# One more K pair of every SwiGLU up strip by seven products instead of eight: four pairs, at groups 5, 7, 10 and 12, where there were three

## The reference

```python
def swiglu(x, w_up, w_down):
    g, u = jnp.split(x @ w_up, 2, axis=-1)
    return (jax.nn.silu(g) * u) @ w_down

h = h + 0.5 * rms_norm(swiglu(rms_norm(h, ffn1_pre[l]), ffn1_up[l], ffn1_down[l]), ffn1_post[l])
h = h + rms_norm(mix, mix_post[l])
h = h + 0.5 * rms_norm(swiglu(rms_norm(h, ffn2_pre[l]), ffn2_up[l], ffn2_down[l]), ffn2_post[l])
```

## Time and profile before

| | |
|---|---|
| median of 3 runs | 2365.75 us (2365.57 to 2366.02) |
| the profiled execution | 2365.93 us, span 2364.2 us |
| PE busy | 2349.9 us (99%), 10579 matmuls |
| DVE busy | 1823.2 us (77%) |
| ACT busy | 1265.4 us (54%) |
| POOL busy | 207.0 us (9%) |
| DMA | 481.64 MB, mean 204 GB/s |

### The profile page before, as it was taken

The page is one execution under the profiler, slowest core; times in us unless marked ns, Lnnn a source line. Parts: engine busy times, 40 slices in busy tenths (PEclk is TensorE's granted clock), DMA queues, the critical chain, the costliest instruction groups (busy, mean ns, idle before and its releaser), DMA issues. The chain is left out here.

```text
span 2364.2 us, 34093 instructions
## 1 busy us (share of the span) xinstructions
PE 2349.9 (99%) x10579; PEld 1938.5 (82%) x10579; DVE 1823.2 (77%) x2163; ACT 1265.4 (54%) x1519; POOL 207.0 (9%) x402
## 2 busy tenths in 40 slices
PE   9999999999999999999999999999999999999998
PEld 7888888888888888888888888888888888888887
DVE  5999999978876655656675767665799999997886
ACT  6555555555545554454555544544655555555553
POOL 1212112110000000000000000000021212111000
PEclk9999999999999999999999999999999999999999
DMA  7666676665676565565565566666666666666665
GB/s 236 218 212 206 216 222 215 220 214 192 207 242 210 159 182 172 160 188 158 178 200 192 195 195 203 194 240 198 204 210 225 213 214 207 218 213 214 205 204 196
DMA packets 267183, 481.64 MB, mean 204 GB/s; under 512 B 21217, under 2 KB 54673, under 8 KB 265457
## 3 DMA queue, kind: packets, MB, share of 16 engines
q1 hardware_dynamic: 252752, 453.04, 59.5%
q0 software_dynamic: 14192, 27.73, 3.5%
q10 hardware_dynamic: 176, 0.07, 0.0%
HBM read 462.93 MB, written 6.29 MB: 198 GB/s over the span
## 5 line engine op out<-in xcount | busy, mean ns | idle before, releaser
L1382 ACT ACTIVATE w_hi<-w_raw 128x1024 fp32r<-128x1024 f32 (+1 forms) x848 | 857.4, 1015 | 926.1 <-PE acc L843 627.9
L1778 DVE TENSOR_TENSOR w_lo<-w_raw,w_hi 128x1024 fp32r<-128x1024 f32 (+1 forms) x848 | 984.2, 1164 | 420.0 <-ACT w_hi L1382 415.5
L841 PE MATMUL acc<-w_hi,xT_hi 128*128 128x512 f32 x1376 | 540.9, 393 | 1.2 <-DVE w_lo L1778 1.0
L843 PE MATMUL acc<-w_hi,xT_lo 128*128 128x512 f32 x1376 | 535.9, 389 | 0.0
L842 PE MATMUL acc<-w_lo,xT_hi 128*128 128x512 f32 x1376 | 535.7, 389 | 0.0
L841 PEld LDWEIGHTS acc<-w_hi,xT_hi 128*128 128x128 f32 x1376 | 258.3, 188 | 56.7 <-issue 3.0
L843 PEld LDWEIGHTS acc<-w_hi,xT_lo 128*128 128x128 f32 x1376 | 258.3, 188 | 54.4
L842 PEld LDWEIGHTS acc<-w_lo,xT_hi 128*128 128x128 f32 x1376 | 258.4, 188 | 52.2
L753 POOL DMA_DIRECT2D act_raw<-blocks x352 | 174.9, 497 | 736.3 <-DVE blocks L2114 646.9
L841 PE MATMUL acc<-w_hi,act_hi 128*128 128x512 f32 x560 | 218.2, 390 | 0.1
L842 PE MATMUL acc<-w_lo,act_hi 128*128 128x512 f32 x560 | 217.9, 389 | 0.0
(11 more groups left out here) (321 smaller groups left out, 2866.0 us busy)
## 6 DMA issues: line engine op xcount, KB each, us to landing
w_raw<-in_ffn_up_dram SPq DMA_DIRECT2D x352, 512.0 KB, 4.2
w_raw<-in_ffn_down_dram SPq DMA_DIRECT2D x176, 512.0 KB, 4.2
w_raw<-in_w_gate_dram SPq DMA_DIRECT2D x96, 512.0 KB, 4.4
w_raw<-in_w_in_dram SPq DMA_DIRECT2D x72, 512.0 KB, 3.7
w_raw<-in_w_in_dram SPq DMA_DIRECT2D x128, 256.0 KB, 3.0
w_raw<-in_w_ret_out_dram SPq DMA_DIRECT2D x32, 512.0 KB, 4.1
w_raw<-in_w_out_dram SPq DMA_DIRECT2D x32, 512.0 KB, 4.5
act_raw<-blocks POOLq DMA_DIRECT2D x352, 32.0 KB, 3.8
```

The costliest lines, as they stand in the source:

```text
L841: pe.matmul(pair[m][:, :], xh, wh, start=(first and kk == 0), stop=False)
L843: mm = pe.matmul(pair[m][:, :], xl, wh, start=False, stop=(last and kk == KG - 1))
L1382: act.activation(w_hi[:, s, cols], w_raw[:, s, cols], ACT.Copy).then_inc(w_rounded, 1)
L1778: dve.tensor_tensor(w_lo[:, s, cols], w_raw[:, s, cols], w_hi[:, s, cols].bitcast(f32), ALU.subtract).then_inc(w_split, 1)
```

## The change

`QUADS` gets a fourth pair, so K pairs 4 to 7 go by seven products, the gate groups standing at 5, 7, 10 and 12 of a pass. The plain groups are reordered: gate groups at 0 to 3, up groups at 4, 9, 14 and 15. The first plain up group, which opens the up half's accumulator, now stands ahead of the first pair, and so the wait for that accumulator moved from the first pair to it. The pair at groups 7 and 8 lies in slots 3 and 0, so the helpers that address its blocks wrap around (`quad_block`, `outer_blocks`, `t_row`). The token sums cover eight K tiles instead of six; `s_hi` moves to the place of `h`, which needs a wait in ScalarE for the store of `h` in the second block. The two places of the sums of weights are used in turn (0, 1, 0, 1).

```diff
-QUADS = ((5, 6, 5), (9, 10, 6), (12, 13, 7))
-PLAIN_GATE = ((0, 0), (1, 1), (2, 2), (3, 3), (4, 4))
-PLAIN_UP = ((7, 0), (8, 1), (11, 2), (14, 3), (15, 4))
+QUADS = ((5, 6, 4), (7, 8, 5), (10, 11, 6), (12, 13, 7))
+PLAIN_GATE = ((0, 0), (1, 1), (2, 2), (3, 3))
+PLAIN_UP = ((4, 0), (9, 1), (14, 2), (15, 3))
...
-        s_hi = sb("s_hi", [P, 4, NQUAD, P], f32r, at=s_x + 16 * NQUAD * P)
+        s_hi = sb("s_hi", [P, 4, NQUAD, P], f32r, at=x_at - 4 * MT * D)
...
-        T_SLOT = (1, 0, 1)
+        T_SLOT = (0, 1, 0, 1)
...
+        PARKED = 16 * MT * 2
...
+        def t_row(j, y):
+
+            swapped = QUADS[j][0] % SLOTS == SLOTS - 1 and y < 2
+            return 1 - y if swapped else y
...
-                for b, tiles in ((2, range(0, 2)), (3, range(2, S_TILES))):
+                for b, tiles in ((2, range(0, 4)), (3, range(4, S_TILES))):
...
-                if first:
-                    pe.wait_ge(acc_read[pair_of(sec, 1)], strip_in_pair(sec, i, 1) + 1)
                 pe.wait_ge(w_split, group(sec, i, nu) + 1 + SLOTS)
                 pe.wait_ge(s_split, f + 1)
-                three(upper[0][:, :], *s(3), *w(nu, 1), first, False).then_inc(w_used, 1)
+                three(upper[0][:, :], *s(3), *w(nu, 1), False, False).then_inc(w_used, 1)
...
+                            if k == 0:
+                                pe.wait_ge(acc_read[pair_of(sec, 1)], strip_in_pair(sec, i, 1) + 1)
...
+                        if f == 1:
+                            act.wait_ge(h_parked, PARKED)
...
-            def quad_blocks(j):
-
-                s = QUADS[j][0] % SLOTS
-                return w_raw[:, s:s + 2, :].rearrange("p s (kk n) -> p (s kk) n", kk=KG)
+            def quad_block(j, y):
+
+                s = (QUADS[j][0] + y // KG) % SLOTS
+                return w_raw[:, s, y % KG * STRIP:(y % KG + 1) * STRIP]
+
+            def outer_blocks(j):
+
+                first, last = [KG * ((QUADS[j][0] + y // KG) % SLOTS) + y % KG for y in (0, 3)]
+                lo, hi = min(first, last), max(first, last)
+                return w_raw[:, :, :].rearrange("p s (kk n) -> p (s kk) n", kk=KG)[:, lo:hi + 1:hi - lo, :]
...
-                dve.wait_ge(t_used, quad(f, i, j) + (2 if j == 0 else 1))
+                dve.wait_ge(t_used, quad(f, i, j) + 1)
                 dve.wait_ge(w_landed[ng % SLOTS], group_landed(sec, i, ng))
                 dve.wait_ge(w_landed[nu % SLOTS], group_landed(sec, i, nu))
-                dve.tensor_tensor(t_pair(t_raw, j, 0), b[:, 0::3, :], b[:, 2:3, :].broadcast_to([P, 2, STRIP]),
+                dve.tensor_tensor(t_pair(t_raw, j, 0), outer_blocks(j), b2.broadcast_to([P, 2, STRIP]),
                                   ALU.add).then_inc(t_summed, 1)
```

More of the change, by code:

```diff
@@ L254, in hybrid_trunk @@
         s_lo = sb("s_lo", [P, 4, NQUAD, P], f32r, at=s_x)
-        s_hi = sb("s_hi", [P, 4, NQUAD, P], f32r, at=s_x + 16 * NQUAD * P)
-        assert s_x + 32 * NQUAD * P <= r_end
+        s_hi = sb("s_hi", [P, 4, NQUAD, P], f32r, at=x_at - 4 * MT * D)
+        assert s_x + 16 * NQUAD * P <= r_end
         h_scaled = sb("h_scaled", [P, S_TILES * P], f32, at=r_hi)
@@ L962, in tt @@
                 def tt(y):
-                    return t_hi[:, T_SLOT[j], y, :], t_lo[:, T_SLOT[j], y, :]
+                    return t_hi[:, T_SLOT[j], t_row(j, y), :], t_lo[:, T_SLOT[j], t_row(j, y), :]
                 if first:
@@ L1121, in swiglu @@
                                     mm = three(acc[pair_of(sec, 1)][m][:, :], xT_hi[:, k + kk, rows], xT_lo[:, k + kk, rows],
-                                               w_hi[:, s, cols], w_lo[:, s, cols], m == 1 and k + kk == 0,
+                                               w_hi[:, s, cols], w_lo[:, s, cols], k + kk == 0,
                                                n == 2 * GD - 1 and kk == KG - 1)
@@ L1592, in swiglu @@
                                 if n == 12:
-                                    wait_quad_used(act, f, NST - 1, 1)
+                                    wait_quad_used(act, f, NST - 1, 2)
                                 hidden_hi(f, n - 12)
@@ L1951, in token_sums @@
                 dve.tensor_tensor(s_raw[:, 3, :, :], a12, s_raw[:, 1, :, :], ALU.add).then_inc(s_summed, 1)
-            def quad_blocks(j):
-                s = QUADS[j][0] % SLOTS
-                return w_raw[:, s:s + 2, :].rearrange("p s (kk n) -> p (s kk) n", kk=KG)
+            def quad_block(j, y):
[5 more added lines that the diff above has]
+                return w_raw[:, :, :].rearrange("p s (kk n) -> p (s kk) n", kk=KG)[:, lo:hi + 1:hi - lo, :]
             def sum13(f, i, j):
                 sec, (ng, nu, k) = f"up{f}", QUADS[j]
-                b = quad_blocks(j)
-                dve.wait_ge(t_used, quad(f, i, j) + (2 if j == 0 else 1))
+                b2 = quad_block(j, 2).rearrange("p (a n) -> p a n", a=1)
+                dve.wait_ge(t_used, quad(f, i, j) + 1)
                 dve.wait_ge(w_landed[ng % SLOTS], group_landed(sec, i, ng))
                 dve.wait_ge(w_landed[nu % SLOTS], group_landed(sec, i, nu))
-                dve.tensor_tensor(t_pair(t_raw, j, 0), b[:, 0::3, :], b[:, 2:3, :].broadcast_to([P, 2, STRIP]),
+                dve.tensor_tensor(t_pair(t_raw, j, 0), outer_blocks(j), b2.broadcast_to([P, 2, STRIP]),
                                   ALU.add).then_inc(t_summed, 1)
             def sum24(f, i, j):
-                b = quad_blocks(j)
                 t = t_raw[:, T_SLOT[j], :, :]
                 dve.wait_ge(t_summed, 3 * quad(f, i, j) + 1)
-                dve.tensor_tensor(t[:, 2, :], t[:, 0, :], b[:, 3, :], ALU.add).then_inc(t_summed, 1)
+                dve.tensor_tensor(t[:, 2, :], t[:, t_row(j, 0), :], quad_block(j, 3), ALU.add).then_inc(t_summed, 1)
                 dve.wait_ge(t_summed, 3 * quad(f, i, j) + 2)
-                dve.tensor_tensor(t[:, 3, :], t[:, 2, :], b[:, 1, :], ALU.add).then_inc(t_summed, 1)
+                dve.tensor_tensor(t[:, 3, :], t[:, 2, :], quad_block(j, 1), ALU.add).then_inc(t_summed, 1)
             def down_sum13(f, i, j):
```

## The result

| | before | after |
|---|---|---|
| median | 2365.89 us (2365.57 to 2367.36, 4 runs) | 2413.82 us (2413.40 to 2415.56, 4 runs) |
| the profiled execution | 2365.93 us, span 2364.2 us | 2413.59 us, span 2411.8 us |

The ratio after to before is 1.0203, with a 95% interval of 1.0185 to 1.0220: slower by 2.0%. Forecast were 2416 us. The first line is the page's busy time by engine, which answers to the earlier trace rows.

The account below looks back on a forecast made before the run. PE bound the kernel before; with the change DVE's list no longer fits under PE and a loop sets the pass. 44.8 + 5.5 = 50.3 us on the 2364.2 us span gave 2414.5, forecast as 2416 us, range 2402 to 2430.

Parts of the forecast that it names:

- The matmuls saved: Up passes: the fourth pair puts 21 matmuls in place of 24; PE alone needs 40.80 us, 0.68 us less a pass.
- DVE no longer fits under PE: Up passes: the pair adds 4.21 us to DVE's 38.81, giving 43.02 us against 40.80 us of PE work.
- The walk: Steps from B (PE's first matmul of group 0) to the next B, forecast at B+43.72, 2.24 us later than before.
- the two decisive `t_lo`: Second `t_lo` of the pairs at 5 and 10, starting at B+16.60 and B+30.72; PE waits 0.8 and 1.9 us.
- the loop: Chain from one B to the next: DVE makes `w_lo` of the next group 3 only after PE has used group 15.
- PE idle of 2.9 us a pass: PE waits for `t_lo` in two places, the third sums' product of the pairs at 5 and 10.
- 44.8 us for 20 passes: Up strips: each pass's next B comes 2.24 us later, over 20 passes.
- 5.5 us for the first passes: Each block's first pass: larger token sums delay `w_lo` of group 4, 2.5 us a block; with transposes 5.5 for both.
- PE stays the bound: Rival for the up passes: DVE catches up, the kernel gets faster, 2353 us; 3 in 100.
- the sides cancel: Rival: PE's saving and DVE's extra balance within 0.2%, a pass of just 41.5 us; 1 in 100.
- Loads late: Rival: loads reach the pairs' sums late, 0.5 to 1.45 us a pass, 2426 to 2445 us; 10 in 100.
- The clock: Rival: waits drop PE to 1.2 GHz, up to 11.6 us a pass; beyond the first passes, 2 in 100.

Follow-up runs that it names:

- e5_free: Kernel after, with `w_lo` of groups 4, 5, 9, 10 and 14 subtracting only 32 of 1024 columns in every pass; 2356.46 us, ratio 0.9956.
- b2_dup4: Kernel before, with four more 128x1024 DVE subtractions in each pass of `up0`, results unread; 2391.87 us against 2367.17 us of before on that chip.
- e2_outside: Kernel after, with `w_lo` of group 15 cut to 32 of 1024 columns, behind the second `t_lo` of the pair at 10; 2413.95 us.
- e8_short: Kernel after, with `w_lo` of the next pass's group 2 cut to 32 of 1024 columns; 2414.05 us, ratio 1.0204.
- e3_inside: Kernel after, with `w_lo` of group 9 cut to 32 of 1024 columns, between the second `t_lo` of the pairs at 5 and 10; 2397.05 us.
- e1_order: Kernel after, with the second `t_lo` of the pairs at 5 and 10 moved ahead of the next pair's sums on DVE; 2424.09 us, ratio 1.0244.
- e9_swap5: Kernel after, with only the second `t_lo` of the pair at 5 moved ahead of the next pair's sums; 2433.56 us, ratio 1.0289.
- e7_both: e1_order with, besides, `w_lo` of the next pass's group 2 cut to 32 columns as in e8_short; 2416.20 us, ratio 1.0214.
- b1_dup2: Kernel before, with two more 128x1024 DVE subtractions in each pass of `up0`, results unread; 2370.08 us against 2367.17 us of before on that chip.
- e4_pool3: e1_order with `sum24` of the pairs at 7, 10 and 12 done by GpSimd instead of DVE; 2520.24 us, ratio 1.0655.
- e6_first: Kernel after, with ACT making `s_hi` one turn later, behind `w_hi` of the next pass's group 3, in each first strip; 2411.80 us.

## Why the prediction was right

- **The matmuls saved, 0.68 us a pass.** Count and size held: 10523 matmuls, and 40.80 us for a pass in e5_free, as forecast.
- **DVE no longer fits under PE.** Held: the pass of 43.63 us less DVE's two waits of 0.30 is 43.03 us; 43.02 was forecast (the window shows 42.72 busy, since it leaves out the short gaps). That a load of this size is enough for the loss, without a fourth pair, is shown by b2_dup4; that the pair costs nothing else is shown by e5_free. The steps of 1.14, 1.33 and 0.60 us were right, and the strided sum costs no more than a plain one: 212.78 to 213.92 for `sum13` of the pair at 10, 204.04 to 205.18 for that of the pair at 7, whose blocks lie in slots 3 and 0; the 0.3 us that the forecast allowed for the stride came from no row. (N+151)/0.96, which it takes from the Trainium skill's page "VectorE: DVE Perf Modes", section "The TRN2 errata", gives nanoseconds and not cycles: 1224 ns for 1024 columns, and the rows have 1.22 us.
- **The walk.** Forecast were B+16.60 and B+30.72 for the two decisive `t_lo`, and B+43.72 for the next B. Measured: B+16.58, B+30.66, B+43.63. That these places bound the pass and not merely lie on the way is shown by e2_outside, e8_short (outside: nothing) and e3_inside (inside: nearly all of it). What the prediction did not say is how near the next bound was. It named DVE's sum only as the lower end of the range; e1_order and e9_swap5 show that with the loads and `t_hi` that a late DVE gets late it lies at 43.4 to 43.9, beside the loop. In the kernel after the two already touch: in some passes of `up1` DVE does not wait at 3' at all (1866.13 and 1909.70). Relieving the loop alone, by the order, buys nothing; e3_inside took work out of both.
- **PE idle of 2.9 us a pass.** The places were right, the way of counting was not. The brackets give 0.70 + 1.52 = 2.2 us. The other 0.6 are the modelled length of the matmul ahead of each wait (0.39 for a step of 0.23) and the slow first one behind it (0.34 to the next start): 2 x (0.16 + 0.11) = 0.54.
- **44.8 us for 20 passes.** It was 42.6: ten of 43.65 - 41.48 = 2.17 us and ten of 43.57 - 41.48 = 2.09. A pass was sized 0.07 to 0.15 us too long, 0.06 of it in DVE's steps up to the pair at 10.
- **5.5 us for the first passes.** The parts in the first strip stood where forecast, as its rows of ACT and DVE show, which answer to the earlier trace rows:

```profile
57.76 1.92 ACT L1580 ACTIVATE s_hi<-s_raw 128x2048 fp32r<-128x2048 f32 x1 [1.71 <-DVE s_raw L1960]
...
60.66 1.23 DVE L1787 TENSOR_TENSOR w_lo<-w_raw,w_hi 128x1024 fp32r<-128x1024 f32 x1 [1.79 <-ACT w_hi L1389]
61.80 2.28 DVE L2150 TENSOR_TENSOR s_lo<-s_raw,s_hi 128x2048 fp32r<-128x2048 f32 x1
...
66.67 1.18 DVE L1787 TENSOR_TENSOR w_lo<-w_raw,w_hi 128x1024 fp32r<-128x1024 f32 x1
```

  `s_hi` was forecast at 57.7, `w_lo` of 4 near 66.8. By the shifts above, the first passes cost 24.4 - 21.7 = 2.7 us in `up0` (2.75 forecast) and 23.3 - 20.9 = 2.4 us in `up1`, 5.1 together. The transposes were priced too high: ACT's `w_hi` behind them, released by PE, starts 0.08 us later (54.99 against 54.91), where 0.27 was forecast.
- **Together.** 42.6 + 5.1 = 47.7 us, where the span grew by 47.6 and 50.3 was forecast. Both terms were a little too large, so the hit is not one error making up for another.
- **The rivals.** *PE stays the bound* and *the sides cancel* did not come. *Loads late*: none in the loop of the kernel after; the thin margin was enough, and a little delay of the list eats it up (e1_order, e7_both, e9_swap5). *The clock*: the forecast priced it as 51 matmuls behind each fall; it is about eight. It fell in one place of the strips of after, in the first pass of `up1` behind the longest wait (granted clock 0.50 from 1753 to 1755 us):

```profile
1751.93 0.50 PE L939 MATMUL bank<-t_hi,s_hi 128*128 128x512 f32 x1 [3.08 <-DVE t_lo L2174]
1752.27 0.44 PE L940 MATMUL bank<-t_lo,s_hi 128*128 128x512 f32 x1
1752.51 0.63 PE L941 MATMUL bank<-t_hi,s_lo 128*128 128x512 f32 x1
1752.93 0.63 PE L939 MATMUL acc<-t_hi,xT_hi 128*128 128x512 f32 x1
...
1766.01 0.50 PE L939 MATMUL bank<-t_hi,s_hi 128*128 128x512 f32 x1
```

  Eight steps of 0.43 us are 1.6 us more, and yet they cost this kernel nothing. The last row is the pair at 10's third sums' product in the same pass, which elsewhere waits 1.5 us; here PE comes to it later and there is no bracket (this is the wait that is missing to 40). A fall behind the wait at the pair at 5 is paid out of the wait at the pair at 10. In e9_swap5 the falls came behind the last wait of a pass, and counted in full. The first pass of `up0` has a wait as long (3.06 us, at 77.98) with no fall behind it.
- **Left open.** Why e7_both gave back 0.4 us a pass and not 0.8 is explained only in part by the waits shown. Whether a correct kernel with four pairs can beat three. None of the orders tried here does; what would be needed is some 3 us of a pass off DVE without GpSimd. ACT, busy for 24.7 of 43.6 us, is where I would look; that wasn't tried.

## What to carry to other kernels

Trading matmuls for vector work pays only up to the point where the vector engine's list for one turn is as long as PE's, and the share on the page does not show that point (77% here, with 2.7 us to spare in 41.5): take a window of one turn. Not even the window's spare time can be spent in full (2.28 us more were too much in b1_dup2). Past it, walk the ring from one turn to the next, and test it by shortening the same instruction inside and outside; but price the engine's plain sum beside it, with the loads that it issues late, before hoping for an order. An idle GpSimd is no relief for float32 tensor_tensor work of a full VectorE.

## What the runs showed of the hardware

- GpSimd's and VectorE's two-input float32 instructions from SBUF exclude each other for their whole length: VectorE's 128x1024 subtraction took 2.30 instead of 1.22 us beside an addition on GpSimd. By form, the half `w_lo` of 128x512 took 1471 ns in the mean between 150 and 237 us of e4_pool3, and 684 ns before.
- TensorE's granted clock fell from 2.4 to 1.2 GHz (0.50) behind waits of 1.8 to 3.1 us, for about eight matmuls, but not behind each of them: once in the 20 passes of after, five times in e9_swap5 (waits of 2.40 to 2.63 us there, with none behind one of 2.69), in both first passes of e6_first (2.18 us), e8_short and e3_inside (3.1 us), and behind waits of 1.83 and 1.90 us in e4_pool3. The waits of 0.6 to 1.5 us of after had no fall behind them. What such a fall costs depends on the next wait: nothing in after and e8_short, where a wait of 1.5 us followed, and 1.6 us each in e9_swap5.
- A VectorE that is a little late costs TensorE time that no bracket shows. In b1_dup2 a pass was 0.26 us longer, 0.2 of it in two steps of 0.33 instead of 0.23 us, with PE busy for all of it.
